# Value rows gathered per token for tiles 0 and 3, one shared pass over the value table for tiles 1 and 2

## The reference, cut to what matters

```python
cand = (s1[..., :, None] + s2[..., None, :])        # 16 x 16 sums of the two half keys' best
top_s, pos = lax.top_k(cand, PEER_TOPK)
eidx = jnp.take_along_axis(cidx, pos, axis=-1)      # i1 * 128 + i2: the expert
g = jax.nn.softmax(top_s, axis=-1)
hid = jax.nn.gelu(einsum('thkd,td->thk', u_tab[eidx], xb)) * g
out = einsum('thk,thkd->td', hid, v_tab[eidx])
```

## Time and profile before

| what | us |
|---|---|
| median of 3 runs | 1875.94 |
| lowest, highest run | 1871.68, 1895.95 |
| span of the profiled execution | 1856.5 |
| start to first dot of tile 0 | 137.65 |
| tile 0's PEER with the pieces of tiles 1 to 3, until | 686 |
| tiles 1, 2, 3 in the loop, each | 391, 387, 386 |

### The profile page before, as it was taken

How to read it: one execution, slowest core, us unless ns; L and a number is a source line. 1 busy time by engine, 2 the same in 40 slices (tenths; PEclk the granted TensorE clock), 3 DMA queues, 4 the chain that set the end, 5 groups by cost and what they waited for, 6 DMA issues and landing times.

```text
span 1856.5 us, 16630 instructions
## 1 busy us (share of the span) xinstructions
PE 1343.4 (72%) x3547; PEld 631.9 (34%) x3547; DVE 1198.2 (65%) x2864; ACT 439.1 (24%) x1049; POOL 1145.1 (62%) x1034
## 2 busy tenths in 40 slices
PE   6976898985588857666666666766777677766776
PEld 5655465572245532222222222222222222222222
DVE  2237768888998766665665566565665666656564
ACT  2323123343332122122121122112121221212112
POOL 0005645663456647777777767777777677777774
PEclk9987987986698988999999999999999999999899
DMA  9449968996689969999999999999999999999997
GB/s 305 152 139 353 348 238 277 322 346 232 229 300 325 345 228 339 347 365 348 342 365 335 347 330 349 351 352 356 347 364 327 338 372 354 365 342 368 340 360 263
DMA packets 196531, 594.24 MB, mean 320 GB/s; under 512 B 18544, under 2 KB 59512, under 8 KB 196472
## 3 DMA queue, kind: packets, MB, share of 16 engines
q0 software_dynamic: 147456, 536.94, 79.0%
q1 hardware_dynamic: 49016, 56.67, 9.3%
HBM read 591.44 MB, written 2.10 MB: 320 GB/s over the span
## 4 chain that ended last, share of the span: by engine, by line
DMA 26%; issue 14%; PE 12%; DVE 10%; POOL 7%; ACT 1%; DVEq 0%; POOLq 0%
DMA v_ring<-in_peer_v_dram,eidx 15%; DMA u_ring<-in_peer_u_dram,eidx 11%; PE acc L730 6%; DVE u_ring L1208 4%; POOL u_ring L507 4%; PE mm L580 3%; POOL v_ring L515 3%; PE acc L580 1%; DVE onehot L1175 1%; DVE picked L1186 1%; DVE onehot L1182 0%; DVE top_p L1165 0%; DVE top_v L1155 0%; DVE top_v L1162 0%; DVE top_hl L1169 0%
## 5 line engine op out<-in xcount | busy, mean ns | idle before, releaser
L730 PE MATMUL acc<-v_ring,diag 128*128 128x512 f32 x1536 | 802.2, 650 | 366.4 <-DMA v_ring<-in_peer_v_dram,eidx 353.6
L1208 DVE CUSTOM_DVE_ANT_0 u_ring<-u_ring,hn 128x1024 f32<-128x1024 f32 x512 | 619.4, 1224 | 388.4 <-DMA u_ring<-in_peer_u_dram,eidx 386.8
L507 POOL DMA_INDIRECT u_ring<-in_peer_u_dram,eidx x512 | 565.8, 1105 | 471.1 <-DVE hid L1208 185.4
L515 POOL DMA_INDIRECT v_ring<-in_peer_v_dram,eidx x512 | 577.2, 1127 | 226.3 <-issue 118.2
L730 PEld LDWEIGHTS acc<-v_ring,diag 128*128 128x128 f32 x1536 | 278.5, 200 | 889.5 <-issue 790.1
L903 ACT ACTIVATE gel<-hid 128x4 f32<-128x4 f32 x128 | 26.2, 205 | 880.1 <-DVE hid L1208 879.9
L1228 DVE SCALAR_TENSOR_TENSOR h<-v_ring,coef,h 128x1024 f32<-128x1024 f32 x128 | 164.4, 1285 | 4.4 <-DMA v_ring<-in_peer_v_dram,eidx 1.0
L910 ACT ACTIVATE diag<-ident,coef 128x128 f32<-128x128 f32 x384 | 131.7, 393 | 91.8 <-PE acc L730 62.3
L580 PE MATMUL mm<-actT,w_ring 128*128 128x384 f32 x336 | 126.1, 534 | 15.9 <-DMA w_ring<-in_w_in_dram 6.3
L580 PEld LDWEIGHTS mm<-actT,w_ring 128*128 128x128 f32 x336 | 69.3, 211 | 67.7 <-issue 20.9
L572 PE MATMUL mm<-w_ring,actT 128*128 128x256 f32 x304 | 77.0, 412 | 1.9 <-issue 0.8
(11 more groups left out here) (192 smaller groups left out, 1055.2 us busy)
## 6 DMA issues: line engine op xcount, KB each, us to landing
w_ring<-in_w_in_dram SPq DMA_DIRECT2D x18, 1024.0 KB, 11.1
w_ring<-in_peer_w_q_dram SPq DMA_DIRECT2D x16, 1024.0 KB, 8.8
u_ring<-in_peer_u_dram,eidx POOLq DMA_INDIRECT x512, 6.1
v_ring<-in_peer_v_dram,eidx POOLq DMA_INDIRECT x512, 6.2
v_ring<-in_w_in_dram SPq DMA_DIRECT2D x6, 1024.0 KB, 12.3
w_ring<-in_w_out_dram SPq DMA_DIRECT2D x6, 1024.0 KB, 11.3
h<-in_x_dram SPq DMA_DIRECT2D x4, 512.0 KB, 6.5
v_ring<-in_w_out_dram SPq DMA_DIRECT2D x2, 1024.0 KB, 5.0
```

What stands on the lines that cost most here:

```text
L507: nc.gpsimd.indirect_dma_start(out=u_ring[:, c % U_RING, :], out_offset=None, in_=peer_u[0], in_offset=bass.IndirectOffsetOnAxis(ap=eidx[p ...
L515: nc.gpsimd.indirect_dma_start(out=v_ring[:, c % V_RING, :], out_offset=None, in_=peer_v[0], in_offset=bass.IndirectOffsetOnAxis(ap=eidx[p ...
L730: last = nc.tensor.matmul(acc[half][:, :], diag[:, c % COLS, :], v_ring[:, c % V_RING, half * BANK:(half + 1) * BANK], start=(starts and c ...
L1208: nc.vector.tensor_tensor_reduce(out=u_ring[:, c % U_RING, :], in0=u_ring[:, c % U_RING, :], in1=hn[:, :], scale=1.0, scalar=0.0, op0=ALU. ...
```

## The change

Tables, attention and results stay the same; the order of the work and the way values are weighed change.

- **Dots.** The 512 gathers of `peer_u` rows and their dots stay. They now come in runs, one per tile, and share one ring of 5 places, `row_ring`, with the gathered value rows (before: 4 and 4).
- **Search.** Two heads are searched together (`topk`, 40 steps), in one go and not woven between dots.
- **Tiles 0 and 3, "swap" and "stripes".** Once all 128 coefficients of a tile are known, indices and coefficients are transposed. A gather then fetches the 128 value rows of one *token*, slot on the partition (`gather_values`). A matmul with a 128x32 stationary operand that is zero but for one column adds the weighted sum to one PSUM row. Four tokens go to four stripes of 32 PSUM rows.
- **Tiles 1 and 2, "spread", "weights", "values".** For every token the matrix of 128x128 expert weights is built as a product of two one-hot matrices on TensorE (`weights`), copied to SBUF by ScalarE (two regions of 64 KB per partition, which hold the attention's data before that). Then the whole value table is read once, in 128 plain loads of 512 KB, and each block is multiplied for both tiles: 4 matmuls of 128x128 by 128x512 (`values`).
- **Order.** One list, ORDER, for all engines. After `query` and `keys` of two heads: tile 0's search and dots go between the other pieces at units 16 to 272 of 647.6; its stripes, one group of four tokens every 6 units, from unit 474.4, since "swap" waits for the last attention (unit 461.4). Then, in order: search of tile 1's first heads, dots 1 (with 5 more searches), dots 2 (with 6 searches and weights 1), weights 2 (with 32 of the dots 3), values 0 to 127, with the other 96 dots 3 at one group of four per three blocks, and stripes 3 from block 88 on, one group per 1.25 blocks; drains and final norms at the end.
- **Host layout.** The weight slabs are handed over so that each partition's 8 KB lie together, and the sub keys transposed, so that the kernel doesn't transpose them.

`add_row`, the diagonal matrices, the second pair of rings and the loops are removed. The core of the diff:

```diff
-COLS = 4
-U_RING = 4
-V_RING = 4
-W_RING = 2
-EARLY_SLABS = 16
+W_RING = 3
+ROWS = 5
+V_SLOTS = 4
+TOKENS = 4
+COLS = 32
+STRIPES = 4
+PACE = 1.0
...
+    QUARTERS = SLOTS // 4
+    first = pieces_of(0)
+    cut_at = first.index(("keys", 0, 1)) + 1
+    rest = first[cut_at:] + pieces_of(1)
+    whole = sum(share(p) for p in rest)
+    attended = sum(share(p) for p in rest[:rest.index(("mix", 1, TILES - 1)) + 1])
+    early = timed(rest, 0.0, PACE * whole)
+    for hp in range(PH // 2):
+        early += [(20.0 * hp, ("topk", 0, hp)), (20.0 * hp + 18, ("gexp", 0, hp))]
+    early += [(16.0 + 8.0 * s, ("dots", 0, s)) for s in range(QUARTERS)]
+    met = max(16.0 + 8.0 * QUARTERS, PACE * attended + 1)
+    early += [(met + 1, ("coef", 0)), (met + 2, ("swap", 0))]
+    early += [(met + 12 + 6.0 * i, ("stripes", 0, i)) for i in range(COLS)]
+    ORDER = first[:cut_at] + [p for _, p in sorted(early, key=lambda e: e[0])]
+
+    def searches(t, hp):
+        return [("topk", t, hp)] + ([("gexp", t, hp - 1)] if hp else [("gexp", t - 1, PH // 2 - 1)] if t > 1 else [])
+
+    ORDER += [("drain", 0)] + searches(1, 0)
+    for s in range(QUARTERS):
+        ORDER += [("dots", 1, s)]
+        if s in (2, 8, 14):
+            ORDER += searches(1, (s + 4) // 6)
+        if s in (20, 26):
+            ORDER += searches(2, (s - 20) // 6)
+    ORDER += [("coef", 1), ("spread", 1)]
+    for s in range(QUARTERS):
+        ORDER += [("dots", 2, s), ("weights", 1, s)]
+        if s in (2, 8):
+            ORDER += searches(2, (s + 10) // 6)
+        if s in (12, 16, 20, 24):
+            ORDER += searches(3, (s - 12) // 4)
+    ORDER += [("gexp", 3, PH // 2 - 1), ("weights_end", 1), ("coef", 2), ("spread", 2)]
+    for s in range(QUARTERS):
+        ORDER += [("weights", 2, s)] + ([("dots", 3, s // 4)] if s % 4 == 3 else [])
+    ORDER += [("weights_end", 2)]
+    done_dots, done_rows = QUARTERS // 4, 0
+    for m in range(K1):
+        ORDER += [("values", m)]
+        if m % 3 == 2 and done_dots < QUARTERS:
+            ORDER += [("dots", 3, done_dots)]
+            done_dots += 1
+            if done_dots == QUARTERS:
+                ORDER += [("scale", 0), ("coef", 3), ("swap", 3)]
+        while done_dots == QUARTERS and done_rows < COLS and m >= 88 + 1.25 * done_rows:
+            ORDER += [("stripes", 3, done_rows)]
+            done_rows += 1
+    ORDER += [("drain", 1), ("scale", 1), ("drain", 2), ("scale", 2)]
+    ORDER += [("stripes", 3, i) for i in range(done_rows, COLS)] + [("drain", 3), ("scale", 3)]
+
...
+        acc = {0: banks[3:5], 1: banks[3:5], 2: banks[5:7], 3: banks[0:2]}
+        turn_bank = {0: banks[6], 1: banks[2], 2: banks[2], 3: banks[2]}
+        w_banks = [banks[0], banks[1], banks[7]]
...
+            def load_values(m):
+                if m < 2:
+                    sp.wait_ge(mm_full, len(MM))
+                elif m < V_SLOTS:
+                    sp.wait_ge(w_full, len(MIXED) * GROUPS_W)
+                else:
+                    sp.wait_ge(v_used, m - V_SLOTS + 1)
+                sp.dma_start(v_slots[m % V_SLOTS], peer_v[0][m * P:(m + 1) * P, :]).then_inc(v_in[m % V_SLOTS], 16)
+
...
-
-            numbers_of(0)
-            for c in range(COLS):
-                gather_u(0, 0, c)
-            for n in range(PH * HOSTS):
-                gathers(n, n % 2, False)
-            with pool.Fori(PH * HOSTS // 2, HEADS // 2 - 1) as i:
-                for par in range(2):
-                    gathers(2 * i + par, par, False)
-            for par in range(2):
-                gathers(HEADS - 2 + par, par, par == 1)
-
+            def gather_scores(t):
+                for c in range(SLOTS):
+                    if c % (2 * TOPK) == 0:
+                        pool.wait_ge(topk_step, TK * (PH // 2 * t + c // (2 * TOPK) + 1))
+                        pool.nop(nofuse=True)
+                    r = row_no("u", t, c)
+                    row_free(r)
+                    nc.gpsimd.indirect_dma_start(
+                        out=row_ring[:, r % ROWS, :], out_offset=None, in_=peer_u[0],
+                        in_offset=bass.IndirectOffsetOnAxis(ap=eidx[:, TILE_SLOT[t], c:c + 1], axis=0)).then_inc(row_in[r % ROWS], 16)
+
+            def gather_values(t):
+                pool.wait_ge(swap_copied, 2 * TURN_ORDER.index(t) + 2)
+                pool.nop(nofuse=True)
+                for c in range(P):
+                    r = row_no("v", t, c)
+                    row_free(r)
+                    at = COLS * (c % STRIPES) + c // STRIPES
+                    nc.gpsimd.indirect_dma_start(
+                        out=row_ring[:, r % ROWS, :], out_offset=None, in_=peer_v[0],
+                        in_offset=bass.IndirectOffsetOnAxis(ap=row_t[:, at:at + 1], axis=0)).then_inc(row_in[r % ROWS], 16)
+
+            gather_scores(0)
+            gather_values(0)
+            for t in range(1, TILES):
+                gather_scores(t)
+            gather_values(TILES - 1)
...
+            def stripes(t, i):
+                k = COLS * GATHERED.index(t) + i
+                pe.wait_ge(pad_done, k + 1)
+                for g in range(STRIPES):
+                    r = row_no("v", t, STRIPES * i + g)
+                    pe.wait_ge(row_in[r % ROWS], 16 * (r // ROWS + 1))
+                    for half in range(2):
+                        last = nc.tensor.matmul(acc[t][half][COLS * g:COLS * (g + 1), :],
+                                                pads[:, g, COLS - 1 - i:2 * COLS - 1 - i],
+                                                row_ring[:, r % ROWS, BANK * half:BANK * (half + 1)],
+                                                start=(i == 0), stop=(i == COLS - 1), skip_group_check=True)
+                    last.then_inc(row_used, 1)
+
+            def weights(t, g):
+                k = GROUPS_W * MIXED.index(t) + g
+                pe.wait_ge(onehot_done, k + 1)
+                pe.wait_ge(scaled, k + 1)
+                if k >= len(w_banks):
+                    pe.wait_ge(w_copied, k + 1 - len(w_banks))
+                for i in range(TOKENS):
+                    last = nc.tensor.matmul(w_banks[k % len(w_banks)][:, i * P:(i + 1) * P],
+                                            picks_c[:, k % 2, i, :], picks_a[:, k % 2, i, :], start=True, stop=True)
+                last.then_inc(w_full, 1)
+
+            def values(m):
+                if m == 0:
+                    pe.wait_ge(w_copied, len(MIXED) * GROUPS_W)
+                    pe.wait_ge(drained, 2)
+                pe.wait_ge(v_in[m % V_SLOTS], 16 * (m // V_SLOTS + 1))
+                for t in MIXED:
+                    for half in range(2):
+                        last = nc.tensor.matmul(acc[t][half][:, :], wts[t][:, m, :], v_slots[m % V_SLOTS][:, BANK * half:BANK * (half + 1)],
+                                                start=(m == 0), stop=(m == K1 - 1), skip_group_check=True)
+                last.then_inc(v_used, 1)
 
...
+                elif kind == "weights":
+                    t, g = p
+                    k = GROUPS_W * MIXED.index(t) + g
+                    act.wait_ge(onehot_done, k + 1)
+                    for i in range(TOKENS):
+                        one = picks_c[:, k % 2, i, :]
+                        at = 2 * P + TOKENS * g + i
+                        last = nc.scalar.activation(one, one, ACT.Copy, scale=tcols[:, at:at + 1])
+                    last.then_inc(scaled, 1)
...
+            def keep_weights(t, g):
+                k = GROUPS_W * MIXED.index(t) + g
+                act.wait_ge(w_full, k + 1)
+                nc.scalar.activation(wts[t][:, :, g * TOKENS:(g + 1) * TOKENS],
+                                     w_banks[k % len(w_banks)][:, :].rearrange("p (t i) -> p i t", t=TOKENS),
+                                     ACT.Copy).then_inc(w_copied, 1)
...
+            def dots(t, quarter):
+                if quarter == 0:
+                    nc.vector.scalar_tensor_tensor(out=hn[:, :], in0=h[:, t, :], scalar=rstd2[:, t:t + 1], in1=g2b,
+                                                   op0=ALU.mult, op1=ALU.mult).then_inc(hn_ready, 1)
+                    dve.wait_ge(hn_ready, t + 1)
+                    if t >= 2:
+                        dve.wait_ge(swap_full, TURN_ORDER.index(t - 2) + 1)
+                for c in range(4 * quarter, 4 * quarter + 4):
+                    r = row_no("u", t, c)
+                    dve.wait_ge(row_in[r % ROWS], 16 * (r // ROWS + 1))
+                    nc.vector.tensor_tensor_reduce(out=row_ring[:, r % ROWS, :], in0=row_ring[:, r % ROWS, :], in1=hn[:, :],
+                                                   scale=1.0, scalar=0.0, op0=ALU.mult, op1=ALU.add,
+                                                   accum_out=hid[:, HID[t], c:c + 1]).then_inc(dot_done, 1)
+
...
+            def fill_pad(t, i):
+                k = COLS * GATHERED.index(t) + i
+                if k > 0:
+                    dve.wait_ge(row_used, STRIPES * k)
```

(23 more changed lines are left out.)

883 lines of the change are left out of this document (401 added, 482 removed).

## The result

The changed kernel takes 2191.5 us (median of 4 runs, 2190.9 to 2196.7), the kernel before 1878.5 (4 runs, 1871.7 to 1896.0): a ratio of 1.166, 95% interval 1.161 to 1.172. The forecast was 2018 us, range 1890 to 2160. The direction is right, the size is not: 173 us are missing, and the time lies outside the range. In spans it is 2194.3 against 1856.5, 338 us more.

What follows compares the result with a forecast made beforehand. It took transfers to bound the old kernel's loop and VectorE its attention stretch. The new kernel's eleven stretches, added in series, gave a span of 1999 us; with 19.4 for the median above the span, 2018 us, range 1890 to 2160.

Steps and rivals of the forecast that it cites:

- D: Swap and stripes 0: 245 us, from 32 groups of four value rows at about 7 us each.
- J: Values 88 to 127 with stripes 3: 262 us, 32 groups at 8.2; bounds 249 and 290.
- B: Units 0 to 272, all dots and searches of tile 0 among the pieces: 262 us; bounds 235 and 285.
- E: Tile 1, 128 dots and 6 searches in one piece each: 280 us; lower bound 246, upper 305.
- F: Tile 2, the same dots and 6 searches, plus weights 1: 287 us; bounds 274 and 315.
- C: Units 272 to 462, attention alone, bound by TensorE: 118 us; bounds 88 and 162.
- A: From the start until the first dot of tile 0: 138 us, as before; bounds 130 and 145.
- G: Weights 2 with 32 dots: 32 groups at 2.5 us, 80 us; bounds 75 and 105.
- H, I, K: Values 0 to 71 with 96 dots, 258 us; values 72 to 87, TensorE alone, 55; the tail, 14.
- Stripes in series: Rival: stripe matmuls run one after another on TensorE, 211 us more, 2229 us; chance 0.12.
- No in-order loss: Rival: each stretch takes only its longest engine or its bytes, 125 us less, 1893 us; chance 0.14.
- The clock: Rival: TensorE's clock at half for a third of values 0 to 87, 100 us more, 2118 us; chance 0.04.

Runs made afterwards that it cites:

- the last experiment: Against the kernel with pads one group ahead: one dot after each weights 2 group, one search moved from tile 0's stripes into tile 1's dots; 1829.7 us, ratio 0.986.

## Why the prediction was right and wrong, step by step

**The failed step: the ring in D and J** (60 + 48 us of 195). The prediction let a group's last row hang on "a chain of three such returns", divided by four groups: three quarters of a return of 7.4 us, and a quarter of the pieces and matmuls, 6.9 in all. That is a chain over rows, as if each place went back while TensorE ran on. But TensorE works in order and in groups: the one row beyond the group in use (issued at 709.60 above) holds its place until that group is done, so of five places only four turn over, and every group waits for one whole return. Its price was too low as well: in D a row was taken up 6.2 us after its issue, where 4.4 was reckoned (J 7.3 for 6.0), and the return came to 9.2 us instead of 7.4. Both belong to the miss: one return of 7.4 would give 7.4 a group, the formula with 9.2 would give 8.3, measured are 9.0 to 9.2. With eight places, where the last row is asked for before the group ahead of it is done, D takes the predicted 245 us: the time was right for a ring that the kernel did not have. That four stripes overlap on TensorE was right.

**The price of a row in B, E and F.** 1.48 us by bytes; 1.6 in truth, from GpSimd's 1.28 + 0.30. The working had "1.25 to 1.4 us per gather" from two issues beside an idle VectorE and took it as hidden. A segment of 24 rows took 38.8 us in E (963.37 to 1002.22) instead of 34: besides the slower rows, the first row after the five in the ring comes some 2 us late. The six segments together are 23 us more, six searches at 0.8 less give 5 back: 18 of E's 20 us. The kernel before could have hinted at it: its mean issue of a score row was 1.1 us over the whole, but 1.22 from 138 to 686 us, which is 1.52 with the 0.30. F is the same step beside a VectorE that is busy 275 of 308 us.

**B and C, 22 us over.** All of it lies in B: from the first dot to the last are 285 us (262 predicted), from there to the last "mix" 117 (118 predicted). VectorE filled 158 of 200 us from 150 to 350, 0.79 and not the 0.88 that the old stretch had. With small dots 31 us went, which holds both VectorE's lighter load and GpSimd's shorter issues; no run parts the two. C was right: 42 GB/s, TensorE busy 44.6 of 50 us.

**A, 12 us over.** The pair's search starts at 129.4, where one head's started at 122.9, and takes 13.7 instead of 9.0. The other 1 to 2 us, and where the expected saving of 5 to 8 us from better packets went, were not tried. Part of the 12 can be scatter: the kernels of the experiments, which leave this stretch alone, have their first dot between 142.5 and 149.2 us.

**Searches: right.** 14.5 predicted, 13.7 measured, and the next dot follows at once:

```profile
897.44 0.87 DVE L1174 MAX8 topk_mem<-region_b 128x8 f32<-128x128 f32 x4
...
911.13 1.22 DVE L1238 CUSTOM_DVE_ANT_0 row_ring<-row_ring,hn 128x1024 f32<-128x1024 f32 x1
```

**G, 19 us over.** The price per group (2.5) was right, as the last experiment shows (2.43). The order of four dots in a row cost 18 us: from the first to the last of VectorE's one-hots are 95 us in the changed kernel and 76 with the dots spread. The prediction added up VectorE's work and did not look at what TensorE had to do while four dots ran.

**H, I, K: right**, to 10, 5 and 2 us. A block takes 248/72 = 3.44 us, TensorE's 4 x 0.86, at a DMA share of 0.91.

**The term outside the span.** 19.4 us were added for what lies around the span. The profiled execution of the changed kernel took 2196.7 us for a span of 2194.3: 2.4 us. The 19.4 were the difference between two executions of the kernel before, whose medians beside these experiments lie between 1853 and 1879. This error hid 22 us of the others.

**The rivals.** Stripes in series: wrong, 16 instructions in 1.94 us; the signature named for it (TensorE never waits in D) is absent as well. The drain at a change of tiling that the Trainium skill names (TensorEngine Tiling (Array Packing), Key Properties) has a small price here (TensorE's timeline in J):

```profile
1997.06 1.88 PE L734 MATMUL bank<-stream,region_a 128*128 128x512 f32 x4
1998.77 1.88 PE L734 MATMUL bank<-stream,region_b 128*128 128x512 f32 x4
2000.58 1.94 PE L710 MATMUL bank<-row_ring,pads 128*32 128x512 f32 x16
2002.46 1.98 PE L734 MATMUL bank<-stream,region_a 128*128 128x512 f32 x4
```

A set of four matmul instructions starts 1.71 us after the one before it. The stripes start 1.81 after theirs, the next set 1.88 after the stripes, and it takes 1.98 instead of 1.88: 0.36 us for the two changes, 11 us over the 32 groups of a stage. It shows where the rows don't bind: without value rows a group of D takes 5.96 us, for 3.7 of pieces and 1.9 of stripes.

No in-order loss: wrong in this kernel; the experiments show that it takes deep rings and pads ahead, and then it nearly holds: D takes its 227 us (with ten searches in it), tile 1 with six searches and twelve places 256 where it had 246. The clock: 1.00 in H, I and most of J. It was 0.50 in tiles 1 and 2, where TensorE had 1 of 300 and 66 of 308 us of work.

**The range.** It took D's upper end from the rival of stripes in series alone. The ring had one formula, 6.9 us a group beside 6.8 by bytes, and no bound above it. By the prediction's own prices a full return in every group, with two more issues ahead of the last row's, is 7.4 + 2.5 = 9.9 us a group in D and 9.0 + 2.5 = 11.5 in J. As upper ends these would have been 32 x 9.9 + 21 = 338 and 32 x 11.5 = 368: the measured 305 and 310 lie under them, and the sum would have had 199 us more room above 2018.

## What to carry over

When one step consumes G buffers at once, count what is in flight while a group is in use: R - G rows of R places. The other 2G - R rows of the next group are asked for only as places come back, so every group waits for a whole round trip of its last row, with up to 2G - R - 1 issues ahead of it. Here that was so at R = 5 and gone at R = 8, with G = 4; nothing between was measured. Look for the head of the line on every in-order engine that feeds the bottleneck: a long search, a wait or a run of dots in front of a 0.2 us copy costs up to its full length, however idle that engine is on the page. A gather's issue is priced beside the work that VectorE does at that time.

## What the runs showed of the hardware

- Four matmuls with 32-column stationary operands in four column stripes ran in the time of one: 16 instructions in 1.94 us, 4 in 1.90. The Trainium skill (TensorE: Matmul & The Clock Gate, Part 3) gives 2.38 times for three; this trace shows 3.9 for four. To change from 128 to 32 columns and back cost 0.36 us.
- The issue of an indirect gather took 938 ns beside an idle VectorE, 1280 beside dots of 1024 columns, 968 beside dots of 128 (means of one kernel each).
- Plain block loads together with gathers moved 408 GB/s, where the kernel before, with gathers alone in its loop, had 349:

```profile
1650.00:1700.00 50.00, 50.00 (x117) 22.06 (x117) 30.23 (x49) 0.00 (x0) 35.44 (x25) 1.00 1.03 408
```
